# The table of chunk rotations of a state-space stage, made with ScalarE's sine of wrapped angles instead of GpSimd's complex products

## What is computed

```
u = h @ w_in                                  # 512 x 1024, seen as 64 groups of 16
step  = exp(log_step)
decay = exp(lam_re * step)
a     = decay * (cos(lam_im*step) + i sin(lam_im*step))     # one complex number for each of 64 x 64 states
x[t]  = a * x[t-1] + (b u)[t]                 # complex recurrence over the 512 positions
y[t]  = Re(c x[t]) + d * u[t]
z     = gelu(y);  val, gate = split(z @ w_glu);  out = val * sigmoid(gate)
```

## Time and profile before

| | |
|---|---|
| Median of 3 runs | 1814.0 us (1813.99 to 1814.23) |
| The profiled execution's own time | 1813.62 us |
| Its span | 1811.9 us |
| Busy: TensorE, VectorE, ScalarE, GpSimd | 97%, 68%, 51%, 29% of the span |
| Mean granted TensorE clock | 0.993 |
| State-space stage | about the first 150 us of the span |

### The profile page before, as it was taken

The page is one execution under the profiler, slowest core; times in us unless marked ns, Lnnn a source line. Parts: engine busy times, 40 slices in busy tenths (PEclk is TensorE's granted clock), DMA queues, the critical chain, the costliest instruction groups (busy, mean ns, idle before and its releaser), DMA issues.

```text
span 1811.9 us, 27470 instructions
## 1 busy us (share of the span) xinstructions
PE 1763.9 (97%) x10262; PEld 1423.5 (79%) x10262; DVE 1238.3 (68%) x1890; ACT 917.1 (51%) x1632; POOL 525.5 (29%) x467
## 2 busy tenths in 40 slices
PE   9989999999999999999999999999999999999997
PEld 6777889999887756678999988778666777866675
DVE  8793478888345767767888845475676676567657
ACT  5423366665224667746565622232566733356763
POOL 7880157675001000005767600032000213200010
PEclk9899999999999999999999999999999999999999
DMA  6222322323333111222232333333211133311111
GB/s 216 82 84 73 103 82 94 117 94 116 105 96 96 45 36 29 62 62 90 95 117 94 115 99 99 95 89 105 64 55 51 47 93 91 102 53 59 47 59 58
DMA packets 58801, 152.61 MB, mean 84 GB/s; under 512 B 17153, under 2 KB 22049, under 8 KB 58673
## 3 DMA queue, kind: packets, MB, share of 16 engines
q1 hardware_dynamic: 55120, 148.21, 26.2%
q0 software_dynamic: 3552, 2.70, 0.6%
HBM read 143.73 MB, written 4.19 MB: 82 GB/s over the span
## 4 chain that ended last, share of the span: by engine, by line
PE 84%; DVE 7%; ACT 4%; POOL 3%; issue 2%; DMA 0%; SPq 0%; ACTq 0%; DVEq 0%; POOLq 0%
PE bank L2406 11%; PE bank L2408 11%; PE bank L2407 11%; PE bank L2608 7%; PE bank L2609 7%; PE bank L2610 7%; PE bank L2964 3%; PE bank L2966 3%; PE bank L2965 3%; PE bank L2917 2%; PE bank L2946 2%; PE bank L2948 2%; PE bank L2947 2%; PE bank L2688 1%; DVE wl L1528 1%
## 5 line engine op out<-in xcount | busy, mean ns | idle before, releaser
L1528 DVE TENSOR_TENSOR wl<-raw,wh 128x1024 fp32r<-128x1024 f32 (+3 forms) x200 | 231.8, 1159 | 271.6 <-ACT wh L844 267.0
L844 ACT ACTIVATE wh<-raw 128x1024 fp32r<-128x1024 f32 (+3 forms) x200 | 194.0, 970 | 355.3 <-PE bank L2408 289.6
L2406 PE MATMUL bank<-hidH,wh 128*128 128x512 f32 x352 | 137.4, 390 | 0.0
L2407 PE MATMUL bank<-hidL,wh 128*128 128x512 f32 x352 | 137.0, 389 | 0.0
L2408 PE MATMUL bank<-hidH,wl 128*128 128x512 f32 x352 | 136.9, 389 | 0.0
L2608 PE MATMUL bank<-xH,wh 128*128 128x256 f32 x480 | 135.8, 283 | 0.0
L2609 PE MATMUL bank<-xL,wh 128*128 128x256 f32 x480 | 135.8, 283 | 0.0
L2610 PE MATMUL bank<-xH,wl 128*128 128x256 f32 x480 | 135.8, 283 | 0.0
L755 POOL TENSOR_TENSOR raw<-raw,wsum 128x512 f32<-128x512 f32 x40 | 86.5, 2163 | 112.2 <-DVE wl L1847 112.2
L2964 PE MATMUL bank<-xH,wh 128*128 128x512 f32 x256 | 111.3, 435 | 6.0 <-ACT qk L1391 3.0
L2966 PE MATMUL bank<-xH,wl 128*128 128x512 f32 x256 | 100.8, 394 | 0.0
(11 more groups left out here) (512 smaller groups left out, 5210.3 us busy)
## 6 DMA issues: line engine op xcount, KB each, us to landing
raw<-w_gu_dram SPq DMA_DIRECT2D x88, 512.0 KB, 3.7
raw<-w_p_dram SPq DMA_DIRECT2D x64, 512.0 KB, 3.6
raw<-w_dn_dram SPq DMA_DIRECT2D x32, 448.0 KB, 3.4
raw<-w_glu_dram SPq DMA_DIRECT2D x16, 512.0 KB, 3.7
raw<-w_dn_dram SPq DMA_DIRECT2D x16, 512.0 KB, 3.6
raw<-w_out_dram SPq DMA_DIRECT2D x16, 512.0 KB, 3.5
raw<-w_in_dram SPq DMA_DIRECT2D x8, 512.0 KB, 7.8
raw<-w_o_dram SPq DMA_DIRECT2D x8, 512.0 KB, 3.5
```

Of the source, the lines that this page charges most:

```text
L844: nc.scalar.activation(wh[:, (st.base + u) % 2, 0:kts * P], raw[:, (st.base + u) % 4, 0:kts * P], ACT.Copy).then_inc(w_high, 1)
L1528: nc.vector.tensor_tensor(wl[:, s, 0:kts * P], raw[:, (st.base + u) % 4, 0:kts * P], wh[:, s, 0:kts * P].bitcast(F32), ALU.subtract).then_ ...
L2406: nc.tensor.matmul(bank, wh[:, s, w], hi[:, k, :], start=first and kt == 0, stop=False)
L2407: nc.tensor.matmul(bank, wh[:, s, w], lo[:, k, :], start=False, stop=False)
```

## The change

`Er` and `Ei` are made as sines. VectorE makes one number for each state, `turn`: 8 x angle in full turns, wrapped (`chunk_turn`, six instructions of 128 x 32, put between the low part of block 1 and `denominator`). GpSimd multiplies `turn` by the chunk number (a column of `vecs`, 0 to 63), and takes off the nearest whole number by adding and subtracting 1.5 x 2^23: four instructions of 128 x 2048 each. ScalarE takes the absolute value, then the sine of pi/2 minus it (the cosine) and the sine, three instructions of 128 x 2048, with one more load of its function table. Removed are all complex products on GpSimd (three at the start, eight in the doubling up to 32 chunks, four upper halves; the diff shows them), and the twelve small instructions of VectorE. All four quarters now wait for the one table. `vecs` grows by 65 columns; `tiny` moves to another place.

```diff
-            cmul(v("p2r"), v("p2i"), v("cos"), v("sin"), v("cos"), v("sin"), v("tpool"))
-            cmul(v("p4r"), v("p4i"), v("p2r"), v("p2i"), v("p2r"), v("p2i"), v("tpool"))
-            cmul(v("u0r"), v("u0i"), v("p4r"), v("p4i"), v("p4r"), v("p4i"), v("tpool"))
-            step(nc.gpsimd.memset(Er[:, :, 0:1], 1.0))
-            step(nc.gpsimd.memset(Ei[:, :, 0:1], 0.0))
             nc.gpsimd.memset(C2[:, :, :, :, :, :], 0.0).then_inc(sem("pool_tables"), 1)
 
-            for turn, n in enumerate((1, 2, 4, 8, 16)):
-                turn %= 2
-                shape = [P, NPAIR, n]
-                wr, wi = (v(f"u{turn}{c}").unsqueeze(2).to_broadcast(shape) for c in "ri")
-                if n == 16:
-                    pool.wait_ge(sem("lrs_ready"), 2)
-                cmul(Er[:, :, n:2 * n], Ei[:, :, n:2 * n], Er[:, :, 0:n], Ei[:, :, 0:n], wr, wi,
-                     tp[:, 0:NPAIR * n].rearrange("p (a b) -> p a b", b=n))
...
-            upper_half(0)
+            shape = [P, NPAIR, NCH]
+            pool.wait_ge(sem("vecs_loaded"), 16)
+            pool.wait_ge(sem("lrs_ready"), 2)
+            each = vecs[:, VEC["chunk"]:VEC["chunk"] + NCH].unsqueeze(1).to_broadcast(shape)
+            whole = column("round").unsqueeze(2).to_broadcast(shape)
+            step(nc.gpsimd.tensor_tensor(Ei[:, :, :], v("turn").unsqueeze(2).to_broadcast(shape), each, ALU.mult))
+            step(nc.gpsimd.tensor_tensor(Er[:, :, :], Ei[:, :, :], whole, ALU.add))
+            step(nc.gpsimd.tensor_tensor(Er[:, :, :], Er[:, :, :], whole, ALU.subtract))
+            nc.gpsimd.tensor_tensor(Ei[:, :, :], Ei[:, :, :], Er[:, :, :], ALU.subtract).then_inc(sem("phases_ready"), 1)
+
             pool.wait_ge(sem("powers_ready"), 1)
             make_t(2)
             pool.wait_ge(sem("sq_used"), KD)
             pool.wait_ge(sd_ready, 1)
             make_v(0)
             pool.wait_ge(sem("v_ready"), 1)
-            upper_half(1)
             make_v(1)
             pool.wait_ge(sem("v_ready"), 2)
-            upper_half(2)
             pool.wait_ge(sem("u_written1"), 64)
             make_t(3)
-            upper_half(3)
...
             act.wait_ge(sem("pool_tables"), 1)
             lag_weights(0)
+            nc.scalar.preload_act_table(ACT.Sin)
+            act.wait_ge(sem("phases_ready"), 2)
+            step(nc.scalar.activation(Er[:, :, :], Ei[:, :, :], ACT.Abs))
             next_block(3)
+            nc.scalar.activation(Er[:, :, :], Er[:, :, :], ACT.Sin, scale=-TURN, bias=tiny[:, 3:4]).then_inc(sem("phases_ready"), 1)
+            nc.scalar.activation(Ei[:, :, :], Ei[:, :, :], ACT.Sin, scale=TURN).then_inc(sem("phases_ready"), 1)
             next_block(4)
...
+            def chunk_turn():
+
+                t, o = v("t"), v("turn")
+                step(nc.vector.tensor_scalar(t, v("sarg"), CH / TWO_PI, None, ALU.mult))
+                step(nc.vector.tensor_scalar(t, t, ROUND, ROUND, ALU.add, ALU.subtract))
+                step(nc.vector.scalar_tensor_tensor(o, t, -PI_A / CH, v("sarg"), ALU.mult, ALU.add))
+                step(nc.vector.scalar_tensor_tensor(o, t, -PI_B / CH, o, ALU.mult, ALU.add))
+                step(nc.vector.scalar_tensor_tensor(o, t, -PI_C / CH, o, ALU.mult, ALU.add))
+                nc.vector.tensor_scalar(o, o, CH / TWO_PI, None, ALU.mult).then_inc(sem("lrs_ready"), 1)
+
...
             split_low(st, 0, 1)
+            chunk_turn()
             denominator()
...
             make_g(0, (1,))
-            dve.wait_ge(sem("phases_ready"), 2)
-            cmul(v("u0r"), v("u0i"), v("u1r"), v("u1i"), v("u1r"), v("u1i"), v("t"))
-            cmul(v("p2r"), v("p2i"), v("u0r"), v("u0i"), v("u0r"), v("u0i"), v("t"))
-            dve.sem_inc(sem("lrs_ready"), 1)
             take_input(3)
...
-                dve.wait_ge(sem("phases_ready"), 3 + q)
+                if q == 0:
+                    dve.wait_ge(sem("phases_ready"), 4)
                 dve.wait_ge(sem("z_made"), q + 1)
```

More of the change, by code:

```diff
@@ L53 @@
 PI_IN = 3.1415925
+TURN = 2 * PI_IN
 VEC = {}
@@ L59 @@
                ("ln_g0", KD), ("ln_g1", KD), ("ln_b0", KD), ("ln_b1", KD), ("q_a", KQ), ("kv_a", KKV), ("q_even", 1),
-               ("q_odd", 1), ("k_head", 1), ("k_rope", 1), ("subln0", 1), ("subln1", 1), ("bf0", 1), ("bf1", 1), ("inv_freq", 1), ("phase", 1)):
+               ("q_odd", 1), ("k_head", 1), ("k_rope", 1), ("subln0", 1), ("subln1", 1), ("bf0", 1), ("bf1", 1), ("inv_freq", 1), ("phase", 1),
+               ("round", 1), ("chunk", NCH)):
     VEC[_n] = _at
@@ L76 @@
 SM = {n: k for k, n in enumerate(
-    "step lrs decay sarg carg sin cos lis t den rden am fr fi r2 r4 r8 p2r p2i p4r p4i tpool u0r u0i u1r u1i".split())}
+    "step lrs decay sarg carg sin cos lis t den rden am fr fi r2 r4 r8 turn".split())}
 HEAD = 64
@@ L194, in build @@
     vecs = everywhere.tensor("vecs", [P, NVEC])
-    tiny = everywhere.tensor("tiny", [P, 64])
     xH = shared.tensor("xH", [P, KD, S], F32R)
@@ L214, in build @@
     minus_unit = everywhere.tensor("minus_unit", [P, P], F32R)
+    tiny = everywhere.tensor("tiny", [P, 64])
     causal = common.tensor("causal", [P, P], F32R)
@@ L649, in v @@
                 return sm[:, SM[name], :]
[L651 to L657, removed]
             pool.wait_ge(sem("factors_ready"), 2)
@@ L672, in _ @@
-            for turn, n in enumerate((1, 2, 4, 8, 16)):
-                turn %= 2
-                shape = [P, NPAIR, n]
-                wr, wi = (v(f"u{turn}{c}").unsqueeze(2).to_broadcast(shape) for c in "ri")
-                if n == 16:
-                    pool.wait_ge(sem("lrs_ready"), 2)
-                cmul(Er[:, :, n:2 * n], Ei[:, :, n:2 * n], Er[:, :, 0:n], Ei[:, :, 0:n], wr, wi,
-                     tp[:, 0:NPAIR * n].rearrange("p (a b) -> p a b", b=n))
[L680 to L689, removed]
-            upper_half(0)
+            nc.gpsimd.memset(C2[:, :, :, :, :, :], 0.0).then_inc(sem("pool_tables"), 1)
@@ L1560, in _ @@
             step(nc.vector.memset(tiny[:, 0:1], EPS))
+            step(nc.vector.memset(tiny[:, 3:4], math.pi / 2))
             nc.vector.memset(tiny[:, 1:2], LN_EPS).then_inc(sem("tiny_ready"), 1)
@@ L3212 @@
         put(f"bf{n}", g["b_forget_2"][n])
+    put("round", np.full(P, ROUND))
+    vec[:, VEC["chunk"]:VEC["chunk"] + NCH] = np.arange(NCH)
     put("kvin", g["kv_in_norm"])
```

## The result

The changed kernel takes **1825.67 us** (median of 4 runs, 1824.76 to 1826.38), the kernel before, run beside it, 1814.12 us. The ratio is 1.0059, with a 95% interval from 1.0045 to 1.0073: it is slower by 0.6%. The profiled execution has a span of 1823.2 us against 1811.9 us before, 11.3 us more.

The account below looks back on a forecast made before the run. TensorE is busy 97%, but early on VectorE, without slack, and GpSimd's table carry the chain. 17.0 + 6.2 - 3.4 - 3.5 - 3.8 = +12.5 us gave a forecast of 1826.5 us, range 1816 to 1836.

Parts of the forecast that it names:

- delay of VectorE at the `Cz` sums: From 16 to 33 us VectorE's small two-SBUF-input instructions stand outside GpSimd's four long ones: +17.0 us, `chunk_turn` included.
- second collision: From 50 us GpSimd's eleven 128x1024 instructions meet ten VectorE ones with two SBUF inputs, 0.75 us each: +6.2 us.
- twelve small ones and the wait for the table gone: VectorE's twelve small instructions and the start behind them removed, -3.4 us; its wait for GpSimd's table gone, -3.5 us.
- start of the turn back: VectorE's first turn back, at 64.5 us before, was to begin at 80.8 us, without a wait on ScalarE.
- later quarters: Fewer VectorE losses to `make_t(3)` and the `V`, -4.3 us, new meetings +0.5: -3.8 us, TensorE following VectorE.
- The rule of turns: GpSimd and VectorE with two SBUF inputs take turns, one whole instruction at a time, also at 2048 columns.
- The first and the third rival: First: long instructions do not keep VectorE out, 1804.6 us, chance 0.13; third: VectorE loses 8, not 17 us, 1818.0, 0.06.
- rival 2: TensorE, idle 13 us, stays at low clock through blocks 2 to 4: +6 us, 1832.5 us, chance 0.07.
- ScalarE** at nothing: ScalarE's table load and three instructions, 7.1 us, cost nothing on the path, covered by VectorE's delay.

Follow-up runs that it names:

- pieces: Changed kernel with each of GpSimd's four 128x2048 table instructions cut into eight of 128x256, 32 in all: 1822.48 us, ratio 1.0037.
- five_long: Changed kernel with the rounding's addition made twice, so five long GpSimd instructions in place of four: 1829.27 us, ratio 1.0074.
- spare_beside_banks: Changed kernel plus two unread GpSimd products of 128x1024 where VectorE turns back, reading banks: 1826.48 us, ratio 1.0068.
- one_round: Changed kernel with the rounding in one single-input GpSimd instruction with two constants, in place of two with two inputs: 1826.15 us, ratio 1.0061.
- The hold: Changed kernel with GpSimd waiting for quarter 0's sums before make_t(2), so its factors run beside VectorE's turn back: 1818.22 us, ratio 1.0019.
- no_sines: Changed kernel with ScalarE's two sines left out, table load and absolute value kept: 1825.41 us, ratio 1.0058.

## Why the prediction held, step by step

| step of the prediction | forecast | measured |
|---|---|---|
| delay of VectorE at the `Cz` sums | +17.0 | +14.4 |
| second collision, above the 1.3 lost before | +6.2 | +6.6 |
| twelve small ones and the wait for the table gone | -6.9 | -6.9 |
| start of the turn back | 80.8 | 78.61 |
| later quarters | -3.8 | -2.8 (what is left of 11.3 after 14.1) |
| sum | +12.5 | +11.3 of span |

The range held, and so did the mechanism. That the sum lies only 1.2 us off is in part luck: the first term was 2.6 us too high, the second 0.4 and the later quarters 1.0 us too low.

**The rule of turns** was the whole of the mechanism, and it held at twice the length that the rows before had shown. `pieces`, `five_long` and `spare_beside_banks` each changed one side of it: a shorter hold, one hold more, a hold beside rows that read a bank. The first and the third rival fell with it. What the Trainium skill says in "SBUF — State Buffer", in its section on the two separate sides (exclusive, and for the whole instruction), agrees with the rows of the changed kernel, 3.50 us for 0.19; it does not agree with `one_round`, whose instruction of 7.10 us let VectorE in once.

**The mis-sized term** is the first. Of the two bounds for the four instructions, 15.6 and 18.8 us, I took a value near the upper, since I put the difference between 2.02 and 2.35 down to the operation, sum against product. It is the operand: a sum with a spread operand took 3.60 us, the difference of two full tensors 4.55. The lower bound, 15.6, was right: 3.66 + 3.60 + 3.65 + 4.55 = 15.5 us. From this alone come the 2.2 us by which the table was ready earlier (31.79 and not 34.0) and 2.0 of the 2.6. The other 0.6 us are many small amounts between there and the end of the `Cz` sums: VectorE's rows, up to 0.1 us longer before beside GpSimd's short instructions (1.51 for 1.42 at the `Cz` sums, 1.32 for 1.23 at the low part), now stand beside an idle GpSimd.

**Second collision.** The total was right by 0.4 us, the even 0.75 for each was not: the meetings cost from 0 to 1.83 us. The hold's 7.4 us fit the sum.

**TensorE** idled 9.9 us, not 13, and rival 2 did not come: behind 37.52 a product row takes 0.63 us, as at 1.2 GHz in the earlier trace rows, and 0.39 from 40.58 on. The rival's nearest trace is the caution above: in single executions the low clock did cost VectorE about 2.4 us, for a while. (Its price of up to 11 us was set too low: before, products begin 0.43 us apart at 72.26 and 0.23 us apart at full speed, so 16.4 us of them would take 14 us more.) Its idle time was VectorE's delay less the lead that it had, so it shrank with the first term.

**ScalarE** at nothing: held, by `no_sines`, by the absence of a wait at 78.61 and by the high part at 53.04.

**Later quarters.** VectorE gained more than was booked. From the first turn back to the second it took 19.21 us and not 21.87 (64.53 to 86.40 before), since its stop for a bank, behind TensorE's slow rows, is gone. This stop stood before at

```profile
79.49 0.69 DVE L1691 TENSOR_TENSOR T<-bank,R 128x512 f32<-128x512 f32 x1 [2.82 <-PE bank L2408]
```

and the prediction had not booked it in this term; it had booked 0.44 for the row at 84.52, and just that row still lasts 1.68. To the third turn back it took 18.22 and not 19.62, the wait of 1.50 gone. Then the pair of low parts lasts 2.36 and not 4.54, of which 0.99 returns as a wait for a bank:

```profile
128.59 2.36 DVE L1508 TENSOR_TENSOR wl<-raw,wh 128x1024 fp32r<-128x1024 f32 x2
131.93 1.42 DVE L1548 TENSOR_TENSOR tv<-bank,Er 128x512 f32<-128x512 f32 x2 [0.99 <-PE bank L2476]
```

In all VectorE gained 5.2 us between its first and its last turn back. Less reached the end. The last quarter's `states`, at 128.64 for 3.25 us above, were before:

```profile
118.63 2.10 PE L2487 MATMUL bank<-U,WM 128*64 128x64 f32 x64 [2.40 <-DVEq L1769]
```

They start 10.0 us later than before, so up to here TensorE did follow VectorE, 4.1 us of the 14.1 gained. But they last 1.15 us longer, at a granted clock of 0.60 where it was 1.00, and the gain on the low parts does not reach TensorE: together 11.2 us, about the 11.3 of the span. "TensorE follows VectorE in these quarters" was the sentence that failed, for the last of them, at a price of about 1 us in this execution. No run isolated it, and where the low clock falls is not the change's doing alone: in the profile of `no_sines` the same row, at 128.63, takes 2.10 us, and that of the quarter before 3.69.

## What to carry to other kernels

An instruction moved to GpSimd is not free because GpSimd is idle: look at what VectorE executes in the same microseconds, and put GpSimd's long instructions beside VectorE rows that read a bank. Where they have to stand beside small ones with both inputs in SBUF, short ones do less harm than long ones. Two such collisions, taken away one by one, gave 7.4 and 8.6 us (the second figure less the work that went to VectorE), and taken away together turned a kernel that was 0.6% slower into one 0.25% faster than before, with the sines kept.

## What was not expected of the hardware

- A VectorE instruction with a single input was shut out as well: the `TENSOR_SCALAR` of 128x32 at 23.73 lasted 3.47 us. The rows before had shown it only for two inputs in SBUF. The Trainium skill ("SBUF — State Buffer", the section on who interferes with whom) counts this operation among those that can take both port pairs, and the row agrees. The `RECIPROCAL` at 19.83, with one input too, lasted 0.35 us as before; it began together with GpSimd's row, so whether it is exempt stays open.
- GpSimd's price goes by the kind of operand: at 128x2048 3.6 us with a spread one, whether product, sum or difference, and 4.55 us with two full tensors. Its one-input instruction with two constants was the slowest, 7.10 us, and the only one of these long ones that let VectorE in before its end.
- A long instruction of either engine holds up the other: 4.19 us for 2.29 on VectorE, then 4.07 for 2.02 on GpSimd.
